# State-space mixer of a 1-core kernel: context end states by a tree, fnet and z panels placed among the input products, 32 coupled steps, outputs with operands exchanged

## What is computed

```
hl = rmsnorm(xl) * (1 + scale) + shift;  hc = rmsnorm(ctx) * (1 + scale_c) + shift_c
p  = hl @ w_in          # 2048 wide: u 768, fnet 256, z 1024
uc = (hc @ w_in)[:, :768]
# per group and direction:
lam_bar = exp(lam * step);  b_bar = (lam_bar - 1) / lam * b
s[t]  = lam_bar * s[t-1] + b_bar @ u[t]        # context first, then latent
y     = Re(c @ s_forward) + Re(c @ s_backward) + d * u
ya = gelu(y);  ya = ya * sigmoid(ya @ glu_w + glu_b)
yb = fft2(fnet part).real @ f_w
out = concat(ya, yb) * silu(z) @ w_out
```

## Time and profile before

| | us |
|---|---|
| three runs | 2802.86, 2807.91, 2811.12 |
| median | 2807.91 |
| profiled execution, its own time | 2810.82 |
| its span (first to last instruction) | 2809.0 |
| mean granted TensorE clock over it | 0.944 of full |

### The profile page before, as it was taken

How to read it: one execution, slowest core, us unless ns; L and a number is a source line. 1 busy time by engine, 2 the same in 40 slices (tenths; PEclk the granted TensorE clock), 3 DMA queues, 4 the chain that set the end, 5 groups by cost and what they waited for, 6 DMA issues and landing times.

```text
span 2809.0 us, 35900 instructions
## 1 busy us (share of the span) xinstructions
PE 2644.7 (94%) x12852; PEld 2175.9 (77%) x12852; DVE 1479.7 (53%) x2488; ACT 931.2 (33%) x1453; POOL 987.6 (35%) x631
## 2 busy tenths in 40 slices
PE   6999999899999999999999899999999898979998
PEld 6878787587778777788787798778888788677786
DVE  5555545755656446444546476543333565934443
ACT  3222224443422124232224565442222333143222
POOL 1978855003759534323524010450000521210310
PEclk9999999998999999999999999999999876859999
DMA  6345446102444462434433210363332335334231
GB/s 176 94 118 146 122 115 177 25 21 61 142 119 122 149 142 84 127 104 141 142 98 84 81 45 1 107 171 97 98 94 85 106 113 118 125 101 124 69 96 60
DMA packets 435043, 295.09 MB, mean 105 GB/s; under 512 B 28947, under 2 KB 414794, under 8 KB 431466
## 3 DMA queue, kind: packets, MB, share of 16 engines
q1 hardware_dynamic: 416810, 212.38, 26.9%
q0 software_dynamic: 18112, 81.08, 9.8%
HBM read 274.07 MB, written 22.50 MB: 106 GB/s over the span
## 4 chain that ended last, share of the span: by engine, by line
PE 74%; DVE 8%; POOL 6%; ACT 4%; issue 3%; DMA 3%; SPq 0%; DVEq 0%; ACTq 0%; POOLq 0%
PE ps L730 55%; PE ps L746 3%; PE ps L898 2%; DVE wl L1915 2%; ACT wh L1423 2%; PE ps L1330 1%; POOL NS L2680 1%; POOL SW L2682 1%; PE ps L889 1%; PE ps L1024 1%; PE ps L1374 1%; POOL NS L2679 1%; PE ps L907 1%; PE ps L1224 1%; DMA raw<-in_ffn_w_gu 1%
## 5 line engine op out<-in xcount | busy, mean ns | idle before, releaser
L1915 DVE TENSOR_TENSOR wl<-raw,wh 128x1024 fp32r<-128x1024 f32 x370 | 613.2, 1658 | 949.9 <-ACT wh L1423 946.9
L1423 ACT ACTIVATE wh<-raw 128x1024 fp32r<-128x1024 f32 x385 | 408.1, 1060 | 1418.8 <-PE ps L730 1325.7
L730 PE MATMUL ps<-XH,wh 128*128 128x512 f32 x1872 | 738.3, 394 | 15.2 <-DVE wl L1915 15.2
L730 PE MATMUL ps<-XH,wl 128*128 128x512 f32 x1872 | 730.7, 390 | 0.0
L730 PE MATMUL ps<-XL,wh 128*128 128x512 f32 x1872 | 730.7, 390 | 0.0
L730 PEld LDWEIGHTS ps<-XH,wh 128*128 128x128 f32 x1872 | 352.8, 188 | 99.6 <-DVE wl L1915 23.0
L730 PEld LDWEIGHTS ps<-XH,wl 128*128 128x128 f32 x1872 | 353.0, 189 | 74.2 <-issue 1.9
L730 PEld LDWEIGHTS ps<-XL,wh 128*128 128x128 f32 x1872 | 352.7, 188 | 74.5
L730 PE MATMUL ps<-HH,wh 128*128 128x512 f32 x704 | 280.9, 399 | 9.1 <-DVE HL L1934 8.6
L730 PE MATMUL ps<-HH,wl 128*128 128x512 f32 x704 | 276.9, 393 | 0.0
L730 PE MATMUL ps<-HL,wh 128*128 128x512 f32 x704 | 276.8, 393 | 0.0
(11 more groups left out here) (453 smaller groups left out, 3772.6 us busy)
## 6 DMA issues: line engine op xcount, KB each, us to landing
raw<-in_ffn_w_gu SPq DMA_DIRECT2D x176, 512.0 KB, 3.8
raw<-in_ffn_w_down SPq DMA_DIRECT2D x64, 512.0 KB, 4.1
AW<-in_ada_w POOLq DMA_DIRECT2D x24, 1024.0 KB, 7.3
raw<-in_ffn_w_down SPq DMA_DIRECT2D x32, 384.0 KB, 3.4
BS<-s_b POOLq DMA_DIRECT2D x12, 1024.0 KB, 7.1
raw<-in_odd_w_in SPq DMA_DIRECT2D x24, 512.0 KB, 3.7
raw<-in_even_w_in SPq DMA_DIRECT2D x22, 512.0 KB, 4.0
raw<-in_w_out SPq DMA_DIRECT2D x16, 512.0 KB, 4.6
```

The costliest lines, as they stand in the source:

```text
L730: mm = pe.matmul(ps[:, p % 4, 0:n], w[:, p % 2, k * P:(k + 1) * P], x[:, k, 0:n], start=(k == 0 and a == 0), stop=(k == nk - 1 and a == 2))
L1423: act.activation(wh[:, p % 2, :], raw[:, p % 4, :], ACT.Copy).then_inc(w_hi, 1)
L1915: dve.tensor_tensor(wl[:, p % 2, :], raw[:, p % 4, :], wh[:, p % 2, :].bitcast(F32), ALU.subtract).then_inc(w_lo, 1)
```

## The change

1. Context products of tiles 0 to 3 are issued inside ffn3, one tile in each of its hooks 0 to 3, without dummies; tiles 4 and 5 in the norm behind it, with dummies. The eight squares of the rms norm get a dummy each. The copies of tiles 4 and 5 stand behind the rms norm on ACT and DVE.
2. The context recurrence on DVE goes. POOL forms the powers `L16` to `L128` of lam_bar^8 by squaring and combines neighbouring chunks of `HC` in five levels (16, 8, 4, 2, 1 pairs), for two tiles at once (`context_end`): pairs 0 and 1 in ffn3, pair 2 behind the low parts of the norm. The result is `HFIN`.
3. `BS` tiles 3 to 6 are fetched in ffn3, 7 and 8 after the norm.
4. The latent shuffle moves from POOL's queue to SP's: after load j + 4 the write of panel j, after load j + 5 its gather in eight transfers.
5. After eight panels PE runs fnet, then the 24 groups of latent products with one 128-row step of z panels 8, 9 or 10 behind each (`z_step`), then panels 11 to 15.
6. DVE merges each odd chunk with the one before it, a tile at a time between the copies (`combine`), then runs 32 steps of two chunks with `L16`, then fills in the others per tile in the tail.
7. Taps and responses have their operands exchanged: inputs and states (64 columns) are stationary, weights (128 columns) move; two groups go to the two column halves of the array and to partitions 0 to 63 and 64 to 127 of the output. ACT copies the result to `YV`, PE turns it round by eight transposes per tile, and gelu reads PSUM in two halves. The round trip through DRAM goes. Taps, responses and transposes of the tiles are issued alternately; the low parts from tile 3 on stand among DVE's state copies.
8. POOL makes five `wl` beside the recurrence (even 13 to glu 1), and its fetches of taps and response weights follow the new order.

The diff, cut to its core:

```diff
+            def u_out(j):
+
+                sp.wait_ge(*taken_at("even", j))
+                sp.dma_start(scratch["s5_u"][j * P:(j + 1) * P, :, NCC:], UT[:, j]).then_inc(shuffle_out[j % 2], 16)
+
+            def u_in(j):
+
+                sp.wait_ge(shuffle_out[j % 2], 16 * (j // 2 + 1))
+                gs = slice(j * GT, (j + 1) * GT)
+                for t in range(L):
+                    sp.dma_start(U[t * S5H:(t + 1) * S5H, gs], u_rows[t][:, gs, NCC:]).then_inc(shuffle_in, 16)
+            for j in range(16):
+                load("even", j, 0, even[:, :, j * P:(j + 1) * P])
+                if 4 <= j < 10:
+                    u_out(j - 4)
+                if 5 <= j < 11:
+                    u_in(j - 5)
...
-            def context_b(t):
+            def context_b(t, warm=False):

                 pe.wait_ge(*b_slot(t))
                 if t == 0:
-                    pe.wait_ge(shuffle_in, 16 * L)
+                    pe.wait_ge(cx_in, 32 + 16 * 6 + 16 * L)
                     pe.wait_ge(cx_f, 8)
                 wait(pe, h_act, t - 1)
                 wait(pe, h_dve, t - 1)
                 for r in range(2):
-                    keep_warm()
+                    if warm:
...
-            ffn("ffn3", nothing)
+            ffn("ffn3", lambda f: context_b(f) if f < 4 else None)
             norm("ffn3", context_b_beside)


             for d in range(KD):
-                if d in (2, 4):
-                    context_b(1 + d // 2)
+                keep_warm()
                 rms_square("even", d)
-            context_b(4)
             rms_root("even")
-            context_b(5)
-            panels("even", 10, split_at("even"))
-
-            pe.wait_ge(shuffle_in, 2 * 16 * L)
-            for t in range(S5T):
-                pe.wait_ge(*b_slot(S5T + t))
-                for b in range(4):
-                    pe.wait_ge(h_act, S5T + (4 * (t - 1) + b + 1 if t > 0 else 0))
-                    pe.wait_ge(h_dve, S5T + (4 * (t - 1) + b + 1 if t > 0 else 0))
-                    for g in range(4):
-                        e = (b % 2) * 4 + g
-                        mm = pe.matmul(ps[:, 4 + b, g * NCL:(g + 1) * NCL], BS[:, t % 3, b // 2, e, :], U[:, t * GT + e, :], start=True, stop=True)
-                    mm.then_inc(b_ps, 1)
-            for j in range(10, 16):
-                panel("even", j, 0, XH, XL)
+            panels("even", 8, split_at("even"))
...
+            def z_step(n):
+
+                j, k = 8 + n // KD, n % KD
+                p = BASE["even"] + j
+                if k == 0:
+                    pe.wait_ge(w_lo, p + 1)
+                    pe.wait_ge(taken[p % 4], p // 4)
+                for a, (w, x) in enumerate(((wh, XH), (wl, XH), (wh, XL))):
+                    mm = pe.matmul(ps[:, p % 4, :], w[:, p % 2, k * P:(k + 1) * P], x[:, k, :], start=k == 0 and a == 0, stop=k == KD - 1 and a == 2)
+                if k == KD - 1:
+                    mm.then_inc(pe_panel, 1)
+
             for t in range(S5T):
+                pe.wait_ge(*b_slot(S5T + t))
+                for b in range(4):
+                    pe.wait_ge(h_act, S5T + (4 * (t - 1) + b + 1 if t > 0 else 0))
+                    pe.wait_ge(h_dve, S5T + (4 * (t - 1) + b + 1 if t > 0 else 0))
+                    for g in range(4):
+                        e = (b % 2) * 4 + g
+                        mm = pe.matmul(ps[:, 4 + b, g * NCL:(g + 1) * NCL], BS[:, t % 3, b // 2, e, :], U[:, t * GT + e, :], start=True, stop=True)
+                    mm.then_inc(b_ps, 1)
+                    z_step(4 * t + b)
+            for j in range(11, 16):
+                panel("even", j, 0, XH, XL)
...
+                for g in range(GT // 2):
+                    for q in range(2):
+                        e = 4 * q + g
+                        mm = pe.matmul(ps[q * S5P:(q + 1) * S5P, 4 + t % 2, g * P:(g + 1) * P], U[:, t * GT + e, :], MM[:, t % 2, e, :],
+                                       start=g == 0, stop=False)
                 mm.then_inc(m_ps, 1)
...
+            def y_t(t):
+
+                pe.wait_ge(y_sb, t + 1)
+                if t == 0:
+                    for j in (14, 15):
+                        pe.wait_ge(*taken_at("even", j))
+                if t == 1:
+                    pe.wait_ge(y_sb, t + 1)
+                if t >= 2:
+                    pe.wait_ge(ya_ready, t - 1)
+                for e in range(L):
+                    mm = pe.transpose(ps[0:S5P, T_BANK[t % 2] + e // 4, (e % 4) * P:(e % 4 + 1) * P], YV[:, t % 2, e].rearrange("p g h -> p (g h)"), IDENT[:])
+                mm.then_inc(yt_ps, 1)
+
+            taps(0)
+            taps(1)
+            responses(0)
+            responses(1)
+            for t in range(S5T):
+                y_t(t)
+                if t + 2 < S5T:
+                    taps(t + 2)
+                    responses(t + 2)
...
-                act.wait_ge(sp_in[j % 2], IN["y"] + 16 * (j // 2 + 1))
-                act.activation(YA[:, j, :].rearrange("p (c t) -> p t c", t=L), YT[:, j % 2], ACT.Gelu_apprx_tanh).then_inc(ya_ready, 1)
+                act.wait_ge(yt_ps, j + 1)
+                for q in range(2):
+                    half = ps[0:S5P, T_BANK[j % 2]:T_BANK[j % 2] + 2, :].rearrange("p b (t m) -> p (b t) m", m=P)[:, :, q * NCL:(q + 1) * NCL]
+                    ins = act.activation(YA[q * S5P:(q + 1) * S5P, j, :].rearrange("p (c t) -> p t c", t=L), half, ACT.Gelu_apprx_tanh)
+                ins.then_inc(ya_ready, 1)
                 act.wait_ge(ya_ready, j + 1)
...
+            def combine(t, first, n):
+
+                gs = slice(t * GT, (t + 1) * GT)
+                x, y = H[:, first:first + NCL - 1:2, :, gs], H[:, first + 1:first + NCL:2, :, gs]
+                re, im = (L8[:, a:a + 1, :, gs].broadcast_to([P, NCL // 2, 2, GT]) for a in range(2))
+                m0, m1 = bulk(0, NCL // 2, GT), bulk(1, NCL // 2, GT)
+                wait(dve, scan, n)
+                dve.tensor_tensor(m0, x, re, ALU.mult).then_inc(scan, 1)
+                dve.tensor_tensor(m1, x, im, ALU.mult).then_inc(scan, 1)
+                dve.wait_ge(scan, n + 1)
+                dve.tensor_tensor(y, y, m0, ALU.add).then_inc(scan, 1)
+                dve.wait_ge(scan, n + 3)
+                dve.tensor_tensor(y, y, m1[:, :, ::-1], ALU.add).then_inc(scan, 1)
+
...
+                if t % 2:
+                    rest(BASE["even"] + 10 + t // 2)
+                dve.wait_ge(h_act, S5T + 4 * t + 4)
+                dve.wait_ge(h_dve, S5T + 4 * t + 4)
+                combine(t, 1, 4 * t)
+            dve.tensor_copy(H[:, 0:1].rearrange("p o r g -> p (o r) g"), HFIN).then_inc(scan, 1)
+            with dve.Fori(0, NCL // 8) as i:
                 for k in range(4):
-                    advance(H, 4 * i + k + 1, 6 * NCC + 2, k == 0)
-            dve.wait_ge(scan, 6 * NC + 2)
+                    advance(4 * i + k + 1, k == 0)
...
             for t in range(S5T):
+                combine(t, 0, S_FILL + 4 * t)
                 states(t)
-            for j in range(6):
-                dve.wait_ge(ya_hi, j + 1)
...
+            def context_end(pair):
+
+                gs = slice(pair * 2 * GT, (pair + 1) * 2 * GT)
+                pool.wait_ge(h_act, 2 * pair + 2)
+                pool.wait_ge(h_dve, 2 * pair + 2)
+                for level, power in enumerate(POWERS):
+                    s, count = 2 ** level, NCC // 2 ** (level + 1)
+                    x, y = HC[:, s - 1:NCC:2 * s, :, gs], HC[:, 2 * s - 1:NCC:2 * s, :, gs]
+                    re, im = (power[:, a:a + 1, :, gs].broadcast_to([P, count, 2, 2 * GT]) for a in range(2))
+                    m0, m1 = bulk(0, count, 2 * GT), bulk(1, count, 2 * GT)
+                    pool.tensor_tensor(m0, x, re, ALU.mult)
+                    step(pool.tensor_tensor(m1, x, im, ALU.mult))
+                    step(pool.tensor_tensor(m0, m0, m1[:, :, ::-1], ALU.add))
+                    last = level == len(POWERS) - 1
+                    ins = pool.tensor_tensor(HFIN[:, :, gs].rearrange("p (c r) g -> p c r g", c=1) if last else y, y, m0, ALU.add)
+                    if not last:
+                        step(ins)
+                ins.then_inc(tree, 1)
+                pool.wait_ge(tree, 5 + pair)
+
+            for t in range(3, S5T + 1):
+                pool.wait_ge(b_ps, t - 2)
+                load_b(t)
+                if t == 4:
+                    context_end(0)
+            context_end(1)
...
-            for j in range(6):
-                pool.wait_ge(*taken_at("even", j))
-                pool.dma_start(scratch["s5_u"][j * P:(j + 1) * P, :, NCC:], UT[:, j]).then_inc(shuffle_out, 16)
-            pool.wait_ge(shuffle_out, 2 * 16 * 6)
-            for t in range(L):
-                pool.dma_start(U[t * S5H:(t + 1) * S5H], u_rows[t][:, :, NCC:]).then_inc(shuffle_in, 16)
...
+            pool.wait_ge(sq_used, PE_SQ["even"] + KD)
+            context_end(2)
...
+            rests(BASE["even"] + 13, BASE["glu"] + 2)
```

278 lines of the change are left out of this document (134 added, 144 removed).

## The result

The changed kernel takes 2765.28 us (median of four runs, 2754.98 to 2776.08), the kernel before 2805.39 us in the same comparison: a ratio of 0.9848, 95% interval 0.9825 to 0.9872. It is 40 us faster; the forecast was 2750 (58 us under the median before), in a range of 2729 to 2783. The profiled execution took 2763.34 us, its span 2761.5.

What follows compares the result with a forecast made beforehand. TensorE, busy 94% of the span with weight panels, bounds nearly the whole kernel; five stretches bound the change. 14 - 32 + 2 - 38 - 9 = -63 from 2810.8 gives 2748, stated as 2750 us; range 2729 to 2783.

Steps and rivals of the forecast that it cites:

- E: Recurrence end to full glu panels: DRAM round trip removed, merges and transposes added, PE 6.8 us a tile; -9 us.
- A: Context products of tiles 0 to 3 between ffn3's gap-free panels, all of it path: 4 x 3.42 us, +14 us.
- the rival: Edge costs: ffn3's fills at the lower clock (+12) or ACT-paced squares (+8), 2758 to 2770; chance 0.13 with late tree.
- B: Norm behind ffn3: spread to spread 22.3 us against 51.2, and 3 us for tile 5's copy and wait; -32 us.
- the sixth rival: POOL's tree late, DVE waits before the latent copies, fnet moves: +20, 2770; chance 0.13 together with edge costs.
- C: Input panels to first latent product: six panels 32.9 us, then fnet 20.2 and 0.9; 54.0 against 51.6, +2 us.
- it fits: In the input panels, SP's load, write and gather take about 4.6 us a panel against PE's 5.48.
- The second rival: SP's queue: the gather's wait holds the next load, a panel takes 14.6 us instead of 5.48: 55 us, 2805; chance 0.04.
- D: First latent product to recurrence end: mixed groups at full clock, then 32 steps; 89.3 us against 127.3, -38 us.
- the clock's: Small products between z parts don't earn full clock: +34, 2784; tail alone +27, 2777; chance 0.13.
- the signs named: Expected in the trace, among others: spread to spread about 22 us, no PE idle before first latent product, steps 1.1 alone.
- wrong if: Groups or tail at clock 0.50 with longer stretch, PE idling over 5 us on loads, DVE merges over 1 us.

## Why the prediction was right, and where it was off

Direction and range held, and in every term the work that was to go went; the sum promised 63 us and 43 came in the trace. Each of the five was off in a step of its own, and in E the size was right for a reason that was wrong in part.

- **A, +14 forecast, +17.5.** The products were priced nearly right (3.49 a tile for 3.42). The step that failed is the choice between the two levels: it said that the panels around a tile keep their rate. Behind two tiles the clock was at its lower level for 3.4 us each, which the run without them showed; the rival had it down for all the tiles (+12).
- **B, -32 forecast, -28.** The part between the spreads was -29 and measured -27.5: the eight squares and dummies took 10.4 us, not 9. The 3 us for tile 5's copy were won (the entwined panels start 8.9 us behind the spread, for 11.5 before) and mostly spent again: the two entwined panels took 9.1 us for 8.0, at a mean clock of 0.79 for 0.92, and the first low part 2.20 for 1.24, beside the tree's third pair. I had costed the tree at nothing because POOL was idle; but POOL's work has a price on DVE, and for this pair DVE had no slack. In time it was: it ended at 2280, 25 us ahead of fnet, though it took 15.8 us and not 12.5, so the sixth rival didn't come.
- **C, +2 forecast, +6.7.** The sum of panels and fnet was right to 0.3 us (32.9 and 20.2 + 0.9 against 32.9 and 21 without the slow start). The failing step is "it fits": SP's work for a panel was priced at 4.6 us from eight issues of 3.62, and these took 3.9 to 8.7 here. The kernel with fnet late has 5.3 at most and no wait on PE, so the longest of them goes with the tables' fetch; that it is the cause was not run by itself. The second rival was there in small: 2.75 us of waiting, and 1.8 us of low clock behind it.
- **D, -38 forecast, -30.7.** Groups of 1.58 us (1.54 forecast) at full clock, merges and last copies to the first step 43.5 us behind the first product (43 forecast), POOL's price 10.3 (10.5 forecast): these held. The step that failed is 32 x 1.12: a step in the loop was taken to last as long when every second state is addressed. It took 1.34, 7 us in all; written out it takes 0.82, so the time is lost in DVE's queue and not in the operations.
- **E, -9 forecast, -8.6.** The number is right in part by luck. Column halves do overlap, as forecast, and at the lower clock 64 records of responses took 6.7 us, as priced. But the term had PE set the pace, at the lower clock all along, 6.8 us a tile, with ACT just under it. In the trace the clock was back for the most part from 2436 on, a tile took PE about 4 us, and PE idled for 17 of 41.9 us; ACT and DVE set the pace, in a ring of waits in which ACT stood 7.6 us. A faster PE and an unforeseen ring cancelled out.

Of the rivals, the clock's came out as forecast against: 1.00 in the products. That was the most valuable choice, and the run with the z steps apart shows that it rested on the right thing: with the products alone the same place runs at 0.50. Of the signs named, three failed without any of the "wrong if" coming true: spread to spread took 23.8 us for about 22, PE did idle ahead of the first product (2.75 us), and a step alone took 1.34 us for 1.1.

## What to carry to other kernels

A loop of short dependent operations can be paced by its engine's queue, as it was here: before halving the number of steps, write them out with constant addresses and see what a step costs then. Work that is moved to fill a wait on the critical engine should be compared with the idle time that the same engine has later; here fnet's 22 us left a place with 27 us idle for one where 8 us had been. And an idle POOL is not free room where DVE is the path: beside the recurrence, 10.8 us of its work took 10.3 from DVE; beside ffn3's panels, where DVE has slack, two pairs of the tree and the powers cost at most 0.9.
